# Two halves of the first modulation as rows on TensorE, their chunks streamed past one column of c, in turns with VectorE

## What is computed

```python
c_act = jax.nn.silu(c)                      # (1, 2048)
mod = c_act @ w_ada[l] + b_ada[l]           # (1, 12288), w_ada is 2048 x 12288 f32
sh1, sc1, gt1, sh2, sc2, gt2 = jnp.split(mod[:, None, :], 6, axis=-1)
h = rmsnorm(x, g_mix[l]) * (1.0 + sc1) + sh1
x = x + gt1 * hybrid_mixer(h, w_in[l], ...)
```

## Time and profile before

| | us |
|---|---|
| median of 3 runs | 3171.72 (3167.26 to 3174.96) |
| time of the profiled execution | 3166.84 |
| its span, first to last instruction | 3165.1 |
| TensorE busy | 3109.9 (98%) |
| VectorE busy | 1983.7 (63%) |
| ScalarE busy | 1481.3 (47%) |
| tile 0 starts on TensorE | 21.02 |
| tile 8 starts | 97.18 |
| tile 16 starts | 135.59 |
| tile 24 starts | 175.25 |

### The profile page before, as it was taken

How to read it: one execution, slowest core, us unless ns; L and a number is a source line. 1 busy time by engine, 2 the same in 40 slices (tenths; PEclk the granted TensorE clock), 3 DMA queues, 4 the chain that set the end, 5 groups by cost and what they waited for, 6 DMA issues and landing times.

```text
span 3165.1 us, 38821 instructions
## 1 busy us (share of the span) xinstructions
PE 3109.9 (98%) x14412; PEld 2584.6 (82%) x14412; DVE 1983.7 (63%) x2082; ACT 1481.3 (47%) x1740; POOL 106.8 (3%) x206
## 2 busy tenths in 40 slices
PE   7899999999999999999999999999999999999999
PEld 6777878788888888888888888888888888888887
DVE  4878777876566566766555565646575565565564
ACT  2345445445444444555445435544445444444543
POOL 1211110100000000000000000000000000000000
PEclk7889999999999999999999999999999999999999
DMA  8888787775555555555555545555555555546555
GB/s 327 330 318 326 287 306 258 283 276 179 192 188 189 188 184 188 171 173 178 183 177 190 191 151 187 180 189 181 176 173 169 194 171 195 176 159 196 168 184 191
DMA packets 179989, 658.45 MB, mean 208 GB/s; under 512 B 20080, under 2 KB 20368, under 8 KB 179216
## 3 DMA queue, kind: packets, MB, share of 16 engines
q1 hardware_dynamic: 150992, 550.51, 51.9%
q0 software_dynamic: 28864, 106.08, 9.0%
HBM read 654.41 MB, written 2.10 MB: 207 GB/s over the span
## 4 chain that ended last, share of the span: by engine, by line
PE 95%; DVE 2%; DMA 1%; issue 1%; ACT 0%; SPq 0%; POOL 0%; DVEq 0%; ACTq 0%
PE pg L1019 29%; PE pg L1021 29%; PE pg L1020 29%; PE pm L1054 1%; PE pm L1073 1%; PE pm L1515 1%; DVE R L1636 1%; DMA w_raw<-w 1%; PE pm L1102 1%; DMA R<-w_ada 0%; PE pm L1409 0%; DVE w_lo L1720 0%; PE pm L1145 0%; PE pm L1086 0%; PE pm L1144 0%
## 5 line engine op out<-in xcount | busy, mean ns | idle before, releaser
L1564 DVE TENSOR_TENSOR w_lo<-w_raw,w_hi 128x1024 fp32r<-128x1024 f32 x888 | 1085.7, 1224 | 974.1 <-ACT w_hi L496 969.4
L496 ACT ACTIVATE w_hi<-w_raw 128x1024 fp32r<-128x1024 f32 x888 | 941.0, 1060 | 1336.8 <-PE pg L1021 1316.6
L1019 PE MATMUL pg<-w_hi,hT_hi 128*128 128x512 f32 x3232 | 1289.5, 399 | 45.0 <-DVE w_lo L1720 34.5
L1021 PE MATMUL pg<-w_hi,hT_lo 128*128 128x512 f32 x3232 | 1272.8, 394 | 0.0
L1020 PE MATMUL pg<-w_lo,hT_hi 128*128 128x512 f32 x3232 | 1272.6, 394 | 0.0
L1019 PEld LDWEIGHTS pg<-w_hi,hT_hi 128*128 128x128 f32 x3232 | 616.4, 191 | 175.9 <-issue 39.3
L1021 PEld LDWEIGHTS pg<-w_hi,hT_lo 128*128 128x128 f32 x3232 | 615.3, 190 | 130.9
L1020 PEld LDWEIGHTS pg<-w_lo,hT_hi 128*128 128x128 f32 x3232 | 616.8, 191 | 125.4 <-issue 0.5
L1019 PE MATMUL pg<-w_hi,y_parts 128*128 128x512 f32 x864 | 338.0, 391 | 1.4 <-issue 1.4
L1021 PE MATMUL pg<-w_hi,y_parts 128*128 128x512 f32 x864 | 336.4, 389 | 0.0
L1020 PE MATMUL pg<-w_lo,y_parts 128*128 128x512 f32 x864 | 336.2, 389 | 0.0
(11 more groups left out here) (275 smaller groups left out, 1364.8 us busy)
## 6 DMA issues: line engine op xcount, KB each, us to landing
w_raw<-w SPq DMA_DIRECT2D x1028, 512.0 KB, 3.5
R<-w_ada POOLq DMA_DIRECT2D x196, 512.0 KB, 6.2
R<-mem_T SPq DMA_DIRECT2D x4, 512.0 KB, 9.9
x_rows<-x SPq DMA_DIRECT2D x1, 2048.0 KB, 21.1
R<-mem_T SPq DMA_DIRECT2D x1, 2048.0 KB, 11.0
out<-x_rows SPq DMA_DIRECT2D x4, 512.0 KB, 5.1
con_sb<-con SPq DMA_DIRECT2D x1, 1344.0 KB, 9.1
small_w_sb<-small_w POOLq DMA_DIRECT2D x2, 576.0 KB, 4.5
```

The costliest lines, as they stand in the source:

```text
L496: act.activation(w_hi[:, g % RING, :, :].rearrange("p c n -> p (c n)"), raw[:, g % RING, :], ACT.Copy).then_inc(hi_done, 1)
L1019: pe.matmul(out, hi, w_hi[:, slot, c, :], start=start, stop=False)
L1021: return pe.matmul(out, lo, w_hi[:, slot, c, :], start=False, stop=stop)
L1564: tt(flat(w_lo[:, g % RING, :, :]), raw[:, g % RING, :], flat(w_hi[:, g % RING, :, :]).bitcast(F32), ALU.subtract).then_inc(lo_done, 1)
```

## The change

Half 3 becomes TensorE's as well, and TensorE uses its chunks in another way: one column of `c` is loaded as weights (128 x 1) and the chunk streams past it in two matmuls of 512 columns, so that the sums land as a row on one partition of two PSUM banks. ScalarE copies the row out (`row_out`), and TensorE turns it into columns with eight matmuls over one partition (`row_columns`); VectorE then adds the bias, as for the other halves. The chunks of halves 2 and 3 now alternate in the stream, and each is used one to a tile, after tiles 8 to 23. Because the row takes two banks of PSUM, the transposes of x now turn over two banks, where they had three.

```diff
-PE_HALVES = (1,)
-CHUNKS = [(h, k) for k in range(KD) for h in (0, 1)] + [(h, k) for h in (2, 3) for k in range(KD)]
+PE_HALVES = (1, 3)
+CHUNKS = [(h, k) for a in (0, 2) for k in range(KD) for h in (a, a + 1)]
...
+            def row_out(n):
+
+                act.wait_ge(ada_pe, KD * (n + 1))
+                if n:
+                    act.wait_ge(row_read, n)
+                for b in range(2):
+                    i = act.activation(mod_row[0:1, b * NW:(b + 1) * NW], pm[2 + b][0:1, :], ACT.Copy)
+                i.then_inc(row_sb, 1)
...
+            upto(11)
+            row_out(0)
             for q in range(GT):
                 upto(11 + q // 3)
                 rows_T(0, q, hf_1, False)
...
                 if p == 2:
                     upto(26)
+                    row_out(1)
...
-            def mod_sums(h, k):
+            def mod_row_sums(h, k):
...
+                    pe.wait_ge(row_sb, PE_HALVES.index(h))
                 pe.wait_ge(ada_in[i % ADA_RING], 16 * (i // ADA_RING + 1))
+                for n in range(2):
+                    last = pe.matmul(pm[2 + n][0:1, :], c_act[:, k:k + 1],
+                                     ada_ring[:, i % ADA_RING, n * NW:(n + 1) * NW], start=k == 0, stop=k == KD - 1)
+                last.then_inc(ada_pe, 1)
+
+            def row_columns(h, bank):
+
+                pe.wait_ge(row_sb, PE_HALVES.index(h) + 1)
                 for m in range(AH // P):
-                    last = pe.matmul(out[:, m:m + 1], ada_ring[:, i % ADA_RING, m * P:(m + 1) * P],
-                                     c_act[:, k:k + 1], start=False, stop=k == KD - 1 and m == AH // P - 1)
-                last.then_inc(ada_pe, 1)
+                    i = pe.matmul(pm[bank][:, m:m + 1], mod_row[0:1, m * P:(m + 1) * P], ones[0:1, 0:1],
+                                  start=True, stop=True)
+                i.then_inc(row_read, 1)
...
             for t in range(8):
                 upto(t + 1)
-                mod_sums(1, 2 * t)
-                mod_sums(1, 2 * t + 1)
+                mod_row_sums(1, 2 * t)
+                mod_row_sums(1, 2 * t + 1)
...
             for t in range(8, 16):
                 upto(t + 1)
+                mod_row_sums(3, t - 8)
                 if t <= 10:
                     for q in range(2 * (t - 7), 2 * (t - 7) + 2):
-                        if q >= 3:
-                            pe.wait_ge(hf_done, q - 2)
+                        pe.wait_ge(hf_done, q - 1)
                         rows_T(0, q, xn_1)
             pe.wait_ge(hf_done, GT)
-            ada_sums(0, 0)
+            row_columns(1, 0)
+            ada_sums(0, 1)
             pe.wait_ge(hn_ready, 1)
-            transposes(mk_tok[0], (1, 2), T_ps)
-            upto(20)
             pe.wait_ge(mod_taken, 2)
+            transposes(mk_tok[0], (0, 1), T_ps)
+            for t in range(16, 24):
+                upto(t + 1)
+                mod_row_sums(3, t - 8)
+            pe.wait_ge(T_sb, 2)
             ada_sums(2, 0)
-            upto(23)
-            ada_sums(3, 1)
+            row_columns(3, 1)
             upto(28)
...
-            weighs.update({8 + i: [(2, 2 * i), (2, 2 * i + 1)] for i in range(8)})
-            weighs.update({17 + i: [(3, k) for k in range(16 * i // 6, 16 * (i + 1) // 6)] for i in range(6)})
+            weighs.update({8 + i: [(2, i)] for i in range(KD)})
...
-            upto(11)
-            take_mod(1, 3)
             upto(14)
             mem_heads(0)
             upto(16)
-            take_mod(0, 0)
+            take_mod(1, 0)
+            take_mod(0, 1)
```

More of the change, by code:

```diff
@@ L276, in build @@
         ada_ring = slot(14, ADA_RING, AH)
+        mod_row = slot(0, AH)
         Zx, Zy, Zp = slot(0, TB, NW), slot(2, TB, NW), slot(8, TB, NW)
@@ L1088, in ada_sums @@
                 i.then_inc(acc_read, 1)
-            def mod_sums(h, k):
+            def mod_row_sums(h, k):
                 i = chunk_at(h, k)
-                q, e = HALVES[h]
-                at = VEC["b_ada"][0] + q * KD + e * (AH // P)
-                out = pm[3][:, 0:AH // P]
                 if k == 0:
-                    if h != PE_HALVES[0]:
-                        pe.wait_ge(mod_taken, 1)
-                    pe.matmul(out, ident, vec[:, at:at + AH // P], start=True, stop=False)
+                    pe.wait_ge(row_sb, PE_HALVES.index(h))
                 pe.wait_ge(ada_in[i % ADA_RING], 16 * (i // ADA_RING + 1))
+                for n in range(2):
[4 more added lines that the diff above has]
+                pe.wait_ge(row_sb, PE_HALVES.index(h) + 1)
                 for m in range(AH // P):
-                    last = pe.matmul(out[:, m:m + 1], ada_ring[:, i % ADA_RING, m * P:(m + 1) * P],
-                                     c_act[:, k:k + 1], start=False, stop=k == KD - 1 and m == AH // P - 1)
-                last.then_inc(ada_pe, 1)
+                    i = pe.matmul(pm[bank][:, m:m + 1], mod_row[0:1, m * P:(m + 1) * P], ones[0:1, 0:1],
+                                  start=True, stop=True)
+                i.then_inc(row_read, 1)
             def broadcast(h, bank):
```

17 lines of the change are left out of this document (8 added, 9 removed).

## The result

| | before | changed |
|---|---|---|
| median, us | 3170.68 (3167.26 to 3174.96, 4 runs) | 3194.35 (3190.15 to 3196.01, 4 runs) |
| ratio to before | | 1.0072 (95% interval 1.0057 to 1.0087) |
| time of the profiled execution | 3166.84 | 3196.01 |
| tile 8 starts | 97.18 | 92.37 |
| tile 16 starts | 135.59 | 144.01 |

The changed kernel is slower, by 23.7 us in the median. Tile 24 starts 23.2 us later in the trace, so the front of the program accounts for nearly all of it. The profiled execution, the slowest of its four, loses 5.9 us more after tile 24. That part is 2988 to 2998 us long in the twelve traces of this case; its mean is 2995.5 in the eight kernels that use halves 2 and 3 in turns and 2990.3 in the other four, and what lies behind this is not shown.

What follows compares the result with a forecast made beforehand. TensorE, busy for 98% of the span, was taken to bound the long later part, so a shift of the front shifts the end. Terms of -11.0, +7.5, +3.0 and +11.8 sum to +11.3 on 3171.72: 3183.0 us, range 3174 to 3204.

Steps and rivals of the forecast that it cites:

- stage one: Tiles 0 and 1, bound by transfers before and after: a change of 0.
- stage two: Tiles 2 to 7: 45.2 us against 56.24, a change of -11.0 (-14.4 to -7.0), with transfers last.
- stage three: Tiles 8 to 15: TensorE replaces VectorE as last, 38.4 us against 30.88, +7.5 (+6.9 to +9).
- junction one: Between tiles 15 and 16: row 1's turning and chunk 8 of half 2 add +3.0 (+2.8 to +4).
- stage four and junction two: Tile 16 up to tile 24: 51.5 us against 39.66, +11.8 (+10 to +16); tile 23 leaves VectorE's chain.
- rival (a): The clock does not hold under one column of weights: 3200, up to 3220 us; chance 0.2.
- A streamed chunk: On TensorE, two float32 matmuls of 512 columns take 1.8 us (bounds 1.72 and 2.1).
- The clock under these streams: TensorE's clock holds at 2.4 GHz while 512-column streams pass one column of weights.
- four ordinary steps: In stage two, four tile steps of 6.9 us each, with transfers last.
- long step: In stage two, the step ahead of tile 6, where VectorE normalises x: 10.5 us.
- The marks: Expected trace readings: tile 8 near 86, tile 16 near 135, tile 24 near 187, stage two's DMA share at least 0.95.
- signs of being wrong: Streamed chunk not near 1.8 us, stage two's steps below 6.3 or above 7.6, or something after tile 24 moving by itself.

Runs made afterwards that it cites:

- ring of four: The changed kernel with a ring of four chunks instead of five: 3196.63 us, ratio 1.0084.
- the kernel in turns with h formed early: The changed kernel with its last chunks one tile earlier and the first two quarters of h formed early: 3184.37 us, ratio 1.0051.

## Why the prediction was right, and where it was short

The sign and the mechanism held: VectorE was freed of work where it was last, and TensorE took more for it in the same place. The forecast was 3183.0 with a sum of +11.3; measured was 3194.35, 23.7 us over before, inside the range (3174 to 3204) but 11 us above the forecast. No rival did this. The sum, term by term (measured from tile starts of the two traces; the last column has the same term from the other traces with the changed kernel's instructions in that stage):

| term | forecast | measured | what was off | other traces |
|---|---|---|---|---|
| stage one | 0 | +0.6 | | |
| stage two | -11.0 | -5.4 | mis-sized by 5.6 | -9.0, -8.3 |
| stage three | +7.5 | +9.6 | mis-sized by 2.1 | +9.6, +9.6 |
| junction one | +3.0 | +3.6 | | +3.2, +3.2 |
| stage four and junction two | +11.8 | +14.8 | mis-sized by 3.0 | +13.2, +13.4 |
| up to tile 24 | +11.3 | +23.2 | | |

With the lowest of these the sum would still be 17.6, 6 over the forecast; the rest of the 11.9 comes and goes with the execution. The measured median lies 2 us above the forecast's own bounds (3177 to 3192) and inside the range only by the part that was added for rival (a), which did not come: that much is luck.

*A streamed chunk* was taken at 1.8 us, from a row with full weights and the bound "one column of weights can't cost more to load than 8 columns do". That bound failed. The records themselves lie 1.80 us apart, but with their two ends a chunk costs 2.0 us: 0.2 x 8 is most of stage three's 2.1, and half of stage four's 3.0. With the weights that the row had, stage three took 38.60 us (forecast 38.4) and the median was 11.8 us over before (forecast 11.3, partly by luck: stage two was 2.3 longer and stage four 1.5 shorter). The junctions came out at 10.70 (10.5) and 12.35 (12.3), but with one column they are 10.70 and 12.45 in the ring of four's trace, so these are not the weights' doing. The Trainium skill, "TensorE: Matmul & The Clock Gate", section "LDWEIGHTS (loading the stationary operand)", lets a load's time go with its columns. The rows agree in direction only, 0.08 us for one column and 0.19 for 128, and go the other way for the kernel: what counts is whether the load runs ahead.

*The clock under these streams* held, as taken: 1.00 in stage three, and the steady low level of stage two is gone. Rival (a) is out. But the clock still falls near long waits, and those remained: stage two's cold time stands behind the wait of 3.83 us that ends at 39.23 and the one of 3.86 us ahead of tile 6.

*Stage two.* Forecast 4 x 6.9 + 10.5 + 6.3 + 0.8 = 45.2, measured 50.8. The four ordinary steps came to 29.0 with the transposes' 0.8 taken off (27.6 forecast), of which one is a step of 8.47 us, at 326 GB/s and a share of 0.94 with a wait of 1.83 us for a transfer, where I had used the 388 GB/s of stage one. The long step took 12.1 (10.5), and the step after it 8.9 instead of 6.3, because tile 6 starts cold. That TensorE waits here for what the transfers bring was right: with half of the chunks' bytes taken away stage two falls to 41.6 us, waits and cold tile included. Whether their rate or the turn-round of the ring comes last is open, since a ring of four made the first three steps 1.2 to 1.7 us longer each. The term that failed is the size: behind the long step and its wait of 3.86 us comes a cold tile, 2.4 us in the step that I had taken for the cheapest. Part of the 5.6 is this execution's: two other traces with the same instructions have 47.2 and 47.9 us, with a long step of 10.2 and 11.4 and 8.0 behind it.

*Junction one* is the turning (1.94) ahead of the sum, and chunk 8 of half 2 ahead of the low parts (1.28 us at 141.49), as named. What I hadn't named is that the clock falls during the sum (2.36 us instead of 1.95), so that the transposes behind it take 1.94 us, where the kernel before had 1.07. In the two other traces with these instructions the sum takes 1.95 and the junction 10.70 and 10.71.

*Stage four and junction two.* Of the 3.0, 1.7 lie in the eight tiles, 0.2 each, and 1.3 are the row's turning, 3.08 us against 1.8. In the two other traces the turning takes 1.94, and the whole 52.84 and 53.02 us, 1.3 and 1.5 over the forecast. The chain behind it was right to 0.02 us. That nothing of TensorE's stands beside it any more cost most of what an order of the same work could save: putting tile 23 back into it gave 4.3 to 5.9 us.

The Trainium skill, "TensorE: Matmul & The Clock Gate", section "HAM oscillation — how this bites in real kernels", puts a fall of the clock down to idle gaps between groups of matmuls. The rows agree in part. Tile 6 at 76.15 follows a gap of 3.86 us and runs at 1.2 GHz from its first matmul; in the kernel in turns with h formed early the same tile follows a gap of 3.87 us and starts at 2.4 GHz, and falls 1.5 us later. The turning at 186.77 takes 3.08 us instead of 1.94 with no gap before it at all, only a sum of one-column matmuls; in two other traces it takes 1.94 behind the same sum.

The marks: tile 8 was to start near 86 (92.4), tile 16 near 135 (144.0), tile 24 near 187 (198.5); the DMA share of stage two was to be at least 0.95 (0.87 over the stage, 0.62 in the cold step after the rings had filled); stage three's TensorE never idle (right), VectorE 18 of 38 (20.5 of 40.5). Of the signs of being wrong two came: a streamed chunk near 1.8 us (1.8 between its records, 2.0 with its ends), and no step of stage two above 7.6 (one of 8.47). A third, something after tile 24 that moves by itself, may have: 5.9 us in the trace, unexplained.

Three things stay open. Whether full weights save anything in stage two: it takes 45.7 to 47.5 us in the three traces with them and 46.7 to 50.8 in the five with one column and a ring of five. Whether the transfers' rate or the ring's turn-round comes last there. And why a load of one column isn't taken ahead is not shown, only that it isn't.

## What to carry to other kernels

Before work is moved off an engine that is last, add up the next engine's step in the same stage: VectorE at 3.5 to 3.9 us a tile gave way to TensorE at 4.75, and the balance was lost by moving half of the chunks. A chain between two stages is worth as much as a stage: look what ran inside it before a change puts that ahead of it, and move what the chain needs into the stage before, where an engine has time. A price read from a row is good for that row's form alone, here down to the width of the weights. And before a difference of a few us between two traces is given a cause, look how far stages of the same instructions differ between traces: here up to 3.6 us.
